# One order for the first attention's last pair, high parts first at every stage's input, and the last two groups of an MLP added in one PSUM bank

## The reference, cut to what matters

```python
for i in range(2):                      # first block: x = LN(alpha*x + f(x)), twice a layer
    m = mla(x) if i == 0 else diff_attn(x)
    x = layernorm(ALPHA * x + m)
    x = layernorm(ALPHA * x + square(relu(x @ w_up[i])) @ w_down[i])
for i in range(2):                      # second block: pre-normed with rmsnorm
    x = x + (forgetting_attention if i == 0 else retention)(rmsnorm(x))
    h = rmsnorm(x)
    x = x + (silu(h @ w_g[i]) * (h @ w_u[i])) @ w_out[i]
return rmsnorm(x)
```

## Time and profile before

| | |
|---|---|
| median of 3 runs | 2573.91 us (2573.46 to 2574.46) |
| the profiled execution | 2575.32 us, span 2573.5 us |
| TensorE busy | 2525.0 us, 98% |
| VectorE busy | 1020.0 us, 40% |
| ScalarE busy | 853.4 us, 33% |
| GpSimd busy | 1056.1 us, 41% |
| mean granted clock of TensorE | 0.996 of full speed |

### The profile page before, as it was taken

One profiled execution on the slowest core, in us unless ns is written; L12 is line 12 of the kernel. 1 busy time (PEld: TensorE's weight loads), 2 busy tenths in 40 slices (PEclk: granted clock), 3 DMA queues, 4 the chain that ended last, 5 costly groups with the idle time before them and its releaser, 6 DMA issues.

```text
span 2573.5 us, 32132 instructions
## 1 busy us (share of the span) xinstructions
PE 2525.0 (98%) x12123; PEld 2086.9 (81%) x12123; DVE 1020.0 (40%) x1832; ACT 853.4 (33%) x1222; POOL 1056.1 (41%) x824
## 2 busy tenths in 40 slices
PE   8998999999999999999999999999999999999998
PEld 6777888888888888887888888888877877888887
DVE  5556344457666444445324322224122132322224
ACT  4434222234565222224333322223222222422222
POOL 4222444444333444443332444444433434344443
PEclk9999999999999999999999999999999999999999
DMA  5212333323212222232221322322322222332222
GB/s 170 68 54 66 98 98 98 98 82 110 71 66 74 98 93 95 97 99 82 82 66 66 99 99 98 98 98 97 108 82 82 82 82 66 106 99 93 92 93 81
DMA packets 164588, 230.77 MB, mean 90 GB/s; under 512 B 14086, under 2 KB 130828, under 8 KB 164364
## 3 DMA queue, kind: packets, MB, share of 16 engines
q1 hardware_dynamic: 164492, 229.43, 27.4%
HBM read 227.32 MB, written 2.10 MB: 89 GB/s over the span
## 4 chain that ended last, share of the span: by engine, by line
PE 57%; issue 25%; POOL 15%; DVE 1%; ACT 1%; DMA 0%; POOLq 0%; SPq 0%; DVEq 0%
POOL w_lo L643 15%; PE bank L671 8%; PE bank L669 8%; PE bank L670 8%; PE bank L680 5%; PE bank L682 4%; PE bank L681 4%; PE bank L1409 2%; PE bank L1410 2%; PE bank L1408 2%; PE bank L1434 1%; PE bank L904 1%; PE bank L866 1%; PE bank L1421 1%; PE bank L923 1%
## 5 line engine op out<-in xcount | busy, mean ns | idle before, releaser
L643 POOL TENSOR_TENSOR w_lo<-w_raw,w_hi 128x512 fp32r<-128x512 f32 (+1 forms) x820 | 1055.9, 1319 | 1494.6 <-ACT w_hi L1558 1494.6
L1558 ACT ACTIVATE w_hi<-w_raw 128x2048 fp32r<-128x2048 f32 (+1 forms) x205 | 392.3, 1914 | 638.8 <-PE bank L682 390.4
L669 PE MATMUL bank<-h_hi,w_hi 128*128 128x512 f32 x1472 | 576.4, 392 | 1.4 <-POOL w_lo L643 0.8
L671 PE MATMUL bank<-h_hi,w_lo 128*128 128x512 f32 x1472 | 572.9, 389 | 0.0
L670 PE MATMUL bank<-h_lo,w_hi 128*128 128x512 f32 x1472 | 572.8, 389 | 0.0
L2067 DVE TENSOR_TENSOR x_residual<-x_residual,bank 128x512 f32<-128x512 f32 x496 | 336.3, 685 | 346.9 <-PE bank L682 307.1
L680 PE MATMUL bank<-w_hi,act_hi 128*128 128x512 f32 x952 | 371.4, 390 | 0.0
L682 PE MATMUL bank<-w_hi,act_lo 128*128 128x512 f32 x952 | 370.5, 389 | 0.0
L681 PE MATMUL bank<-w_lo,act_hi 128*128 128x512 f32 x952 | 370.4, 389 | 0.0
L669 PEld LDWEIGHTS bank<-h_hi,w_hi 128*128 128x128 f32 x1472 | 276.4, 188 | 64.5 <-issue 7.4
L670 PEld LDWEIGHTS bank<-h_lo,w_hi 128*128 128x128 f32 x1472 | 276.4, 188 | 57.8 <-issue 1.0
(11 more groups left out here) (249 smaller groups left out, 3044.2 us busy)
## 6 DMA issues: line engine op xcount, KB each, us to landing
w_raw<-in_ffn_w_in SPq DMA_DIRECT2D x44, 1024.0 KB, 5.1
w_raw<-in_ffn_w_up SPq DMA_DIRECT2D x32, 1024.0 KB, 5.4
w_raw<-in_ffn_w_down SPq DMA_DIRECT2D x32, 1024.0 KB, 4.9
w_raw<-in_ret_w_in SPq DMA_DIRECT2D x24, 1024.0 KB, 5.2
w_raw<-in_ffn_w_out SPq DMA_DIRECT2D x22, 1024.0 KB, 4.8
w_raw<-in_diff_w_qkv SPq DMA_DIRECT2D x12, 1024.0 KB, 5.1
w_raw<-in_fox_w_in SPq DMA_DIRECT2D x12, 1024.0 KB, 5.3
w_raw<-in_ret_w_out SPq DMA_DIRECT2D x8, 1024.0 KB, 5.0
```

Of the source, the lines that this page charges most:

```text
L643: nc.gpsimd.tensor_tensor(m.w_lo[:, sl, at], m.w_raw[:, sl, at], m.w_hi[:, sl, at].bitcast(F32), ALU.subtract)\
L669: mm(out, hi, x[0][:, k, :], start=k == 0, stop=False)
L671: last = mm(out, lo, x[0][:, k, :], start=False, stop=k == kc - 1)
L1558: m.nc.scalar.activation(m.w_hi[:, sl, 0:width], m.w_raw[:, sl, 0:width], ACT.Copy).then_inc(m.sem("w_hi_ready"), 1)
```

## The change

It joins several edits:

- mla's last pair gets an order of its own on TensorE, ScalarE and VectorE (`last_rotary_pair`). normalize comes ahead of other work on VectorE, keys(3,1) stand behind the scores of head 6, two output blocks of pair 2 behind them; the output blocks of pairs 2 and 3 follow `DRAIN["mla"]`; the first turn for ffn0 comes ahead of block (1,7). keys(1,0) move ahead of the first scores, and in pairs 0 and 1 VectorE normalizes before some of its takes.
- `pe_input_blocks` computes the products with h_hi first and those with h_lo last, and waits for them apart.
- In the layer norm and the RMS norm, ScalarE's `act_high` of the first half goes ahead of `deviation(2)` or `scale(2)`. In ffn0 ScalarE computes the rotary tables of diff after the split for down([0]) and not before. The high part of ffn0's first weights is made inside the layer norm.
- In an MLP's last two groups, (0, n) and (1, n) accumulate in one bank, and VectorE adds once: 8 additions less in each of ffn0, ffn1, sw0 and sw1.
- At the end, the last tile is squared, scaled and stored in two column halves, the first half scaled by ScalarE (`act_end`, `dve_end`).

```diff
 TAIL = [(0, n) for n in range(4)] + [(1, n) for n in (0, 2, 1, 3)] + [(0, n) for n in range(4, 8)] + [(1, n) for n in range(4, 8)]
-TAIL_BANK = {(which, n): 4 + n if which == 0 and n < 4 else n % 4 for which, n in TAIL}
-TAIL_COUNT = {x: n + 1 for n, x in enumerate(TAIL)}
-TAIL_FREE = {x: max([TAIL_COUNT[y] for y in TAIL[:at] if TAIL_BANK[y] == TAIL_BANK[x]], default=0) for at, x in enumerate(TAIL)}
+TAIL_BANK = (4, 5, 6, 7, 0, 1, 2, 3)
+TAIL_COUNT = {n: at + 1 for at, n in enumerate(n for which, n in TAIL if which)}
 TAIL_ADDS = ((0, 2, 1), (3,), (4, 5), (6, 7))
...
 DRAIN = {
+    "mla": [(0, n) for n in range(8)] + [(1, n) for n in range(8)],
...
 DRAIN_BANK = {
+    "mla": {0: (4, 5, 6, 4, 5, 6, 7, 6), 1: (4, 5, 0, 1, 2, 3, 2, 3)},
...
+MLA_ORDER = [("k0", "k1", "pe", "q0", "q1", "v0", "v1", "v2", "v3"),
+             ("k0", "q0", "q1", "k1", "pe", "v0", "v1", "v2", "v3"),
+             ("q0", "k0", "q1", "k1", "pe", "v0", "v1", "v2", "v3"),
+             ("q0", "k0", "q1", "pe", "v0", "v1", "v2", "v3", "k1")]
...
@@ -719,18 +735,29 @@
 
     s, b, mm = m.sem, m.bank, m.nc.tensor.matmul
     w, cols = weight(m, [unit], 2048, KC), slice(256 * half, 256 * half + 256)
-    for j in range(2):
+
+    def high(j, k):
+        out = b[banks[j]][:, cols]
+        mm(out, w[0][:, k, j * P:(j + 1) * P], m.h_hi[:, k, cols], start=k == 0, stop=False)
+        mm(out, w[1][:, k, j * P:(j + 1) * P], m.h_hi[:, k, cols], start=False, stop=False)
+
+    def low(j):
         for k in range(KC):
             if j == 0 and k % 2 == 0:
-                pe_weights(m, pe, [unit], None, k // 2 + 1)
-                pe.wait_ge(*m.upto(f"{t}_h_hi", 4 * half + k // 2 + 1))
                 pe.wait_ge(*m.upto(f"{t}_h_lo", 4 * half + k // 2 + 1))
-            out, hi, lo = b[banks[j]][:, cols], w[0][:, k, j * P:(j + 1) * P], w[1][:, k, j * P:(j + 1) * P]
-            mm(out, hi, m.h_hi[:, k, cols], start=k == 0, stop=False)
-            mm(out, hi, m.h_lo[:, k, cols], start=False, stop=False)
-            last = mm(out, lo, m.h_hi[:, k, cols], start=False, stop=k == KC - 1)
+            last = mm(b[banks[j]][:, cols], w[0][:, k, j * P:(j + 1) * P], m.h_lo[:, k, cols], start=False, stop=k == KC - 1)
         if half:
             last.then_inc(s("blocks_done"), 1)
+
+    for k in range(0, KC, 2):
+        pe_weights(m, pe, [unit], None, k // 2 + 1)
+        pe.wait_ge(*m.upto(f"{t}_h_hi", 4 * half + k // 2 + 1))
+        for j in range(2 if k < 4 else 1):
+            high(j, k), high(j, k + 1)
+    low(0)
+    for k in range(4, KC):
+        high(1, k)
+    low(1)
...
     def keys(p, j):
         out = b[key_bank(t, p, j)][:, :]
         if t == "mla":
-            if p and j:
+            if p == 1 and j == 0:
+                pe_weights(m, pe, unit("k", p))
+                wait("k_in", 2)
+            elif p == PAIRS - 1 and j:
+                wait("v_in", TT * p + 2)
+            elif p and j:
                 wait("k_in", 2 * p + 1)
...
         if t == "mla":
             if p and tile == 0:
-                wait("k_in", 2 * p + 2)
+                wait("k_in", 2 * p + (1 if p == PAIRS - 1 else 2))
...
+    def turn_input(first_after):
+        wait("acc", drain_turned(t, first_after))
+        beside()
+
+    def last_rotary_pair():
 
         p = PAIRS - 1
         a, c = 2 * p, 2 * p + 1
+        pe_turn(m, pe, t, a - 2)
+        queries(p, 0), keys(p, 0)
+        head_values(a - 2)
+        pe_scores(m, pe, t, a - 1)
+        queries(p, 1), rotated_queries(p)
+        values(p, 0), values(p, 1)
+        pe_turn(m, pe, t, a - 1)
+        values(p, 2), values(p, 3)
+        head_values(a - 1)
+        pe_scores(m, pe, t, a)
+        keys(p, 1)
+        block(0, 0), block(0, 1)
+        pe_turn(m, pe, t, a)
+        block(0, 2)
+        head_values(a)
+        pe_scores(m, pe, t, c)
+        block(0, 3), block(0, 4), block(0, 5)
+        pe_turn(m, pe, t, c)
+        block(1, 0, (0,)), block(1, 1, (0,))
+        head_values(c)
+        block(0, 6), block(0, 7)
+        block(1, 0, (1,)), block(1, 1, (1,))
+        for n in range(2, 7):
+            block(1, n)
+        turn_input((1, 7))
+        block(1, 7)
...
@@ -1635,8 +1675,8 @@
     deviation(0), deviation(1), scale(0), scale(1)
     if first:
         act_split(m, act, [first])
+    act_high(m, act, to, 0)
     deviation(2)
-    act_high(m, act, to, 0)
...
@@ -1656,9 +1696,8 @@
     scale(0), scale(1)
     if first:
         act_split(m, act, [first])
-    scale(2)
     act_high(m, act, t, 0)
-    scale(3)
+    scale(2), scale(3)
...
-    def attend_last():
-        a, c = HEADS - 2, HEADS - 1
+    def last_rotary_pair():
+        p = PAIRS - 1
+        a, c = 2 * p, 2 * p + 1
+        turned(a - 2)
+        split(f"mla.o{p - 1}")
+        head_out(a - 2)
+        exps(a - 1)
+        turned(a - 1)
+        head_out(a - 1)
+        values(p, 0), values(p, 1)
+        exps(a)
+        split(f"mla.o{p}")
         turned(a)
         head_out(a)
         exps(c)
-        head_hi(a)
-        split(after([f"{t}.o{PAIRS - 1}"])[0])
         turned(c)
         head_out(c)
-        head_hi(c)
...
     up([0])
     up([1])
+    down([0])
     if t == "ffn0":
 
         act.wait_ge(*m.upto("mla_pe_in", PAIRS))
         act_rope(m, act, "diff", ROPE_STEPS)
-    down([0])
...
-    act_layernorm(m, act, "ln0", "ffn0", None, "ffn0.u1")
+    act_layernorm(m, act, "ln0", "ffn0", "ffn0.u0", "ffn0.u1")
...
             take("q", 0, 0), take("q", 0, 1), take("k", 0, 0), take("k", 0, 1)
         maxima(0)
         if t == "mla":
-            take("q", 1, 0), take("k", 1, 0)
-        normalize(0)
+            take("q", 1, 0), normalize(0), take("k", 1, 0)
+        else:
+            normalize(0)
...
                 take("k", p, 0)
             maxima(c), head_low(a)
             if p == 1:
-                take("k", p, 1), take("q", p, 1), normalize(c)
+                take("k", p, 1), normalize(c), take_rotated(p), take("q", p, 1)
             else:
-                take("q", p, 1), normalize(c), take("k", p, 1)
-            take_rotated(p), head_low(c)
+                take("q", p, 1), normalize(c), take("k", p, 1), take_rotated(p)
+            head_low(c)
...
+    def drained(which, n):
+        before = DRAIN_COUNT[t][0, n] if which else KC * (PAIRS - 3) + n + 1
+        dve_add_block(m, dve, t, n, b[DRAIN_BANK[t][which][n]], [f"{t}.o{PAIRS - 2 + which}"], n, None, None, False,
+                      which == 1 and t in POST_NORMED, before)
+
+    def last_rotary_pair():
         p = PAIRS - 1
-        a, c = HEADS - 2, HEADS - 1
-        added(p - 1, 3)
-        if t == "diff":
-            maxima(c), head_norm(a)
-        else:
-            head_low(a), maxima(c)
-        for n in range(TT):
-            added(p - 1, TT + n)
-            normalize(c, [n])
-        if t == "diff":
-            head_low(a), head_norm(c)
-        head_low(c)
-        end(by_tile(ROW_ADDS, lambda n: added(p, n, t in POST_NORMED)), rows_complete(PAIRS), lambda n: None)
+        a, c = 2 * p, 2 * p + 1
+        take("q", p, 0), take("k", p, 0)
+        maxima(a - 1), head_low(a - 2), take("q", p, 1), normalize(a - 1), take_rotated(p), head_low(a - 1)
+        maxima(a), take("k", p, 1), normalize(a)
+        drained(0, 0), drained(0, 1), drained(0, 2), head_low(a)
+        maxima(c), normalize(c, [0, 1, 2]), drained(0, 3), normalize(c, [3])
+        drained(0, 4), drained(0, 5), head_low(c), drained(0, 6), drained(0, 7)
+        end(by_tile(ROW_ADDS, lambda n: drained(1, n)), drain_complete(t), lambda n: None)
...
 def dve_last_groups(m, dve, t, groups, sums):
 
-    base = KC * (groups - 2)
-
-    def adder(which):
-        def add(n):
-            before = base + TAIL_COUNT[0, n] if which else base - KC + n + 1
-            dve_add_block(m, dve, t, n, m.bank[TAIL_BANK[which, n]], [f"{t}.d{groups - 2 + which}"], n, None, None, False, sums and which == 1, before)
-        return add
-
-    return adder(0), adder(1)
+    def add(n):
+        dve_add_block(m, dve, t, n, m.bank[TAIL_BANK[n]], [f"{t}.d{groups - 1}"], n, None, None, False, sums, KC * (groups - 3) + n + 1)
+
+    return add
...
+def dve_end(m, dve, add):
+
+    s, v = m.sem, m.nc.vector
+    last = TT - 1
+    row = slice(last, last + 1)
+    for tile in range(last):
+        for n in TAIL_ADDS[tile]:
+            add(n)
+        if tile:
+            dve_rms_tile(m, dve, "out", tile - 1, m.x[:, tile - 1, :], 5)
+    add(2 * last)
+    dve_rms_tile(m, dve, "out", last - 1, m.x[:, last - 1, :], 5)
+    dve.wait_ge(*m.upto("out_first_sq", 1))
+    v.tensor_scalar(m.x_sum[:, 1:2], m.x_sum[:, 0:1], 1.0 / D, RMS_EPS, ALU.mult, ALU.add).then_inc(s("out_first_eps"), 1)
+    v.tensor_tensor(m.x[:, last, 0:512], m.x[:, last, 0:512], m.gain_2[:, 0:512], ALU.mult).then_inc(s("out_gained"), 1)
+    add(2 * last + 1)
+    dve.wait_ge(*m.upto("out_std", TT))
+    v.reciprocal(m.x_rstd[:, row], m.x_std[:, row]).then_inc(s("out_rstd"), 1)
```

(17 more changed lines are left out.)

182 lines of the change are left out of this document (82 added, 100 removed).

## The result

The changed kernel took 2559.41 us (median of 4 executions, 2557.08 to 2561.66) beside 2574.18 for the kernel before on the same chip: ratio 0.9942, 95% interval 0.9928 to 0.9956, 14.8 us faster. The forecast was 2555.9 in 2549 to 2563. The profiled execution took 2561.51 around a span of 2559.7.

The account below looks back on a forecast made before the run. TensorE, busy 98%, was taken to bound the kernel, so only its waits and clock counted. Savings summed to 20.0 us, less 2.0 for clock and hand-overs, 18.0 off the 2573.91 median: 2555.9 us, range 2549 to 2563.

Parts of the forecast that it names:

- the last pair: First attention's last pair and the way into ffn0: 12.0 us of waits and low clock go, 4.2 come, gain 7.8.
- wrong if the first attention saves under 6 us: Sign against the forecast: the prediction called itself wrong if the first attention saved less than 6 us.
- the other sign: Sign against the forecast: the prediction called itself wrong if low-clock spells multiply.
- pair 1: First attention: keys(1,0) ahead of the scores and earlier normalizations shorten TensorE's waits for q, gain 1.7 us.
- diff to ffn1: First half's 2.2 us wait goes but returns as a wait for tile 2; gain 0.7 + 0.8 = 1.5 us.
- tails: Last two groups of each MLP, added in one bank: TensorE's count stays as it was, gain nothing.
- Then what comes: Way into ffn0: new waits at rotated(3), turn(6), the layer norm tiles and the second half, 4.2 us in all.
- minus 2.0: Clock allowance taken from the 20.0 us sum: one low-clock spell costing 1.6 us, and 0.4 for hand-overs.
- Rival one: Clock falls at each new stretch (second turns of ffn0, ffn1, fox), three 3.4 us spells or one of 10: 2559; chance 0.17.
- ffn1 to fox: Way into fox: normed tiles come 2.2 us earlier, but GpSimd's splits for fox.k0 become the bound; gain 3.0 us.
- a lasting low clock: Rival: lower clock granted after ffn0's turn stays, 2580 us at 52 us of it; slower or unseen, chance 0.04.
- each freed wait reappears: Rival: everywhere, each freed wait returns one engine later, leaving 8 us of gain: 2566 us; chance 0.06.

Follow-up runs that it names:

- a0_same: The changed kernel with no edit, run again for its spread and a second trace: median 2560.4 us, ratio 0.9944 to the kernel before.
- b3: The changed kernel with the last two groups of each MLP in two sets of banks again, 32 additions back on VectorE: 2557.0 us.
- a1: The changed kernel with VectorE's addition of output block (1,4) directly ahead of the first layer norm finish instead of behind both: 2556.4 us.
- e1: The changed kernel with block (1,4) added ahead of the finishes and, in fox.k0's first half, all w_hi matmuls ahead of w_lo's: 2551.7 us.

## Why the prediction was right, and where it failed

The time fell in the range, 3.5 us above the number. It was right part by part away from the last pair and fox; for the last pair the account was wrong, and that the total still fell in the range is in part luck and the width of the range. One of the prediction's own signs, "wrong if the first attention saves under 6 us", was escaped only just: from the first matmul to ffn0's second half the profiled execution saved 6.1 us (by the trace's clock 5.7, 233.53 to 227.85, where "near 223" was forecast), a0_same 9.1. Spells did not multiply, the other sign: while TensorE computes, before's trace has three (10.2, 3.4 and, at 1214.8, one of 3.4 that the earlier trace rows does not show), the changed kernel's three (6.8, 3.4, 3.4), a0_same's one, at 1199.4.

- *Right, by place*: pair 1 (1.7; 1.9 by its waits), the rope's order (1.0; 1.1), ffn0 to diff (with the rope 2.4; 2.4), diff to ffn1 (1.5; 1.5, with the wait for tile 2 that was to take the removed wait's place: 1.46, at 816.51 below), fox to sw0 (1.8; 1.8), 0.8 at each later second half (0.7), tails nothing (b3), the end (0.2; 0.5, in its bounds).

```profile
816.51 1.06 PE L729 MATMUL bank<-consts,x_residual 128*128 128x128 f32 x8 [1.46 <-DVE x_residual L2173]
817.81 1.09 PE L729 MATMUL bank<-consts,x_residual 128*128 128x128 f32 x8 [0.24 <-DVE x_residual L2173]
819.03 0.36 PE L741 MATMUL bank<-h_hi,w_hi 128*128 128x256 f32 x1
```

- *The step that failed: "Then what comes", the list of the last pair's new waits, 4.2.* Of its entries rotated (0.9; 0.95) and turn(7) (none; none) held; turn(6) was 0.35 and measured 1.1; of the tiles' 0.75 and the second half's 2.3 only 0.5 came in a0_same and 0.1 in the profiled execution, because one wait stood ahead of them that is not in the list: 3.35 at block (1,6) for bank 2. I said that "TensorE now has (1,2) to (1,6), 6.8 us, to cover two centers and two finishes" and never asked whether (1,6) could be issued before the finishes were over. Without a spell the waits sum to some 5.8 instead of 4.2, and the stretch saved 6.5 instead of 7.8. a1 shows the cause by moving the addition.
- *Mis-sized: "minus 2.0", the clock.* I took one spell of 1.6 and 0.4 for hand-overs. In the profiled execution there were two at the places concerned, 2.4 and 1.3. Without them the kernel saved 18.7 of 20.0 (a0_same, by the table). Rival one (the clock falls at each new stretch, 2559) was nearer than the forecast, though at other places: at the bank and at fox's splits, not at the second turns of ffn0 and ffn1, where TensorE kept its clock here (b3_tails_undone's trace does have a spell at ffn1, 814.7 to 818.1). The Trainium skill, "TensorE: Matmul & The Clock Gate", Part 1 on oscillation, has the lower clock come back with each of a row of long waits. For the single wait of 3.19 us one trace agrees and the other does not.
- *Mis-sized: ffn1 to fox, 3.0.* Its waits for GpSimd were priced at 4.6 and printed as 3.2, but the quarters of fox.k0 took longer than the 7.97 in the earlier trace rows. GpSimd in order of time, and VectorE's operations beside it:

```profile
1161.58 6.09 POOL L659 TENSOR_TENSOR w_lo<-w_raw,w_hi 128x512 fp32r<-128x512 f32 x4 [12.72 <-ACT w_hi L1598]
1168.33 8.63 POOL L659 TENSOR_TENSOR w_lo<-w_raw,w_hi 128x512 fp32r<-128x512 f32 x4 [0.67 <-ACT w_hi L1598]
...
1169.28 2.12 DVE L2173 SCALAR_TENSOR_TENSOR x_residual<-work,x_rstd,tokbuf 128x1024 f32<-128x1024 f32 x1
...
1175.96 2.09 DVE L2148 SCALAR_TENSOR_TENSOR tokbuf<-x_residual,x_rstd,gain 128x1024 f32<-128x1024 f32 x1
```

  The four finishes and scales now follow each other without additions between, so every quarter of the split meets one: 8.63 for four. (A slower quarter beside such an operation is what the traces show side by side; no run took the operations away.) The quarters ended only 1.0 earlier against ffn1's second half than before, where I had 1.7, and the blocks after them met the spell. e1 shows what TensorE's order of the two parts of the weight was worth there, 3.1 us with GpSimd no faster.
- *Wrong attribution, hidden by the sum.* I booked the whole way into ffn0 (waits of 2.46 and 0.85, low clock 2.6) to the last pair because its waits came first in time. Undone, the pair's order costs at most 0.7 by the medians; alone it gains 3.1; the matmul order alone gains 6.0. The pair's order seems worth nothing in the medians because it brings what it has to pay for: 2.9 gained in the stretch, and a wait for a bank behind which a spell of 2.4 can come. Undoing ScalarE's order costs 1.5 into ffn0 (with a spell of 3.4 us) and 0.8 into ffn1 and gives 1.2 back at fox. A forecast of the total could not show this; runs with one part did.
- *The other rivals*: a lasting low clock did not come (longest spell 6.8 while TensorE computes); "each freed wait reappears" held only where VectorE or GpSimd bound anyway, at ffn1 and fox.

## What to carry to other kernels

When an engine is given more blocks to cover another's chain, write beside each block the bank it needs and where in the other engine's queue that bank is emptied; a block whose release stands behind the chain covers nothing. Then look which engine is next: here it was GpSimd's low part of the weight. Where a weight comes as a high and a low part from different engines, give all the high part's matmuls first and the late part's last (shown at fox, 3.1 us). Price parts in stretches that touch the same wait jointly, and test them both alone and undone: the last pair's edit gains 3.1 alone and costs 0 to 0.7 undone.
